# A long convolution's spectrum products shared between VectorE and GpSimd

## The chip, the cores and the metric

The kernel runs on one core of a Trainium2 chip. The metric is the device time of one execution in microseconds, the median of three runs. The kernel is one launch of three transformer-like blocks with a sequence of 512 and a model width of 1024. Below, DVE is VectorE, POOL is GpSimd, ACT is ScalarE, PE is TensorE (PEld its weight loads) and SP the queue that issues the DMAs.

## The reference

Only one step of the second block matters here, the two-sided long convolution of the Hyena mixer. It multiplies, per channel, the spectrum of `u` by the spectrum of a filter, and goes back to time:

```python
def _bidir_fftconv(u, k_fwd, k_bwd):
    L = u.shape[1]
    n = 2 * L
    D = k_fwd.shape[1]
    k_c = jnp.concatenate([k_fwd.at[0].add(k_bwd[0]), jnp.zeros((1, D), jnp.float32), k_bwd[:0:-1]], axis=0)
    kf = jnp.fft.rfft(k_c, n=n, axis=0)
    uf = jnp.fft.rfft(u, n=n, axis=1)
    return jnp.fft.irfft(uf * kf[None], n=n, axis=1)[:, :L]

# in _hyena_mixer
    u = (v * x1).astype(jnp.float32)
    y = _bidir_fftconv(u, k_fwd, k_bwd) + u * skip.astype(jnp.float32)
    y = y.astype(h.dtype) * x0
    return y @ w_out + b_out
```

## The kernel before

Everything around this step is a sequence of stages, each with a block of its own in which the five engines run their own instruction lists and meet through counting semaphores. The stage in question is `hyena_convolution` (line 2036). Its neighbours are `hyena_projection`, which makes `u` and `x0`, and the feed-forward network of the same block, which follows.

Both spectra are made by matrix products with cosine and sine tables. The filter's spectrum is already in `T.spectrum`, a tile of 128 partitions by 2 (q) by 2 (real, imaginary) by 2 (side) by 1024 channels. Even and odd samples are transformed apart, and the two sides of the spectrum are then sum and difference of the two transforms. The stage runs so:

1. PE turns `u` (line 2067), ACT copies it into `ut` (2111).
2. Four rounds n, `ROUNDS[n]` = (half, q): half picks 512 of the 1024 channels, q one of two groups of frequencies. PE makes the four parts of the unit spectrum in four banks (`parts_of_spectrum`, line 1713); rounds 0 and 2 use banks 0 to 3, rounds 1 and 3 banks 4 to 7. ACT copies the even parts out of PSUM into `even` (2118).
3. DVE does all the arithmetic of a round in `multiply(n)` (2142 to 2160). The join (2148) is two instructions that read `even` in SBUF and the odd part in PSUM and write `u`. Then, with all operands in SBUF, come four products of 128x1024 (`rr`, `ii`, `ri`, `ir`, lines 2151 to 2154), the real part `rr - ii` and the imaginary part `ri + ir` (2155, 2156), and four side sums of 128x512 (2158, 2159), which overwrite the filter's spectrum with the product's. There is one `u`, one `rr`, and so on, so the rounds follow one another.
4. PE transforms back (2083): channels 0 to 511 (tiles m of 0 to 3) when rounds 0 and 1 are finished and the join of round 2 has read its banks, channels 512 to 1023 (m of 4 to 7) when rounds 2 and 3 are finished.
5. DVE adds the skip and multiplies by `x0` (`gate`, 2166 and 2170, with `tmp` in between), ACT and DVE split the result into a high and a low part (2133, 2176), ACT and POOL split the output weights (2125, 2104), and PE makes the output product (202 to 204), whose result DVE adds to the residual (2188).

POOL does nothing in this stage but the 16 weight splits of 128x512 at line 2104. At the end of a stage, POOL clears each of its semaphores with an instruction of its own (`stage`, line 139).

Of the kernel before, what the change touches and what calls it, by code (L numbers as in the profile page):

```python
# [7 lines left out]
ALU = mybir.AluOpType  # L8
# [6 lines left out]
P = 128  # L15
SEQ = 512
D = 1024
KT = D // P
# [1680 lines left out]
HALF_D = D // 2  # L1699
# [336 lines left out]
def hyena_convolution(G, T):  # L2036
# [3 lines left out]
    with ExitStack() as ctx:  # L2040
        S = stage(G, "long", ctx, "turned", "copied", "spectra", "even_copied", "step", "joined", "product",
# [3 lines left out]
        u = G.sb("long_spectrum", [P, 2, 2, HALF_D], ctx=ctx)  # L2045
        rr, ii, ri, ir = (G.sb("long_" + n, [P, 2, HALF_D], ctx=ctx) for n in ("rr", "ii", "ri", "ir"))
        tmp = G.sb("long_tmp", [P, 4, SEQ], ctx=ctx)
        w_parts = [G.sb("long_weights_" + part, [P, 2, UNIT // 2], F32R, ctx=ctx) for part in ("high", "low")]
# [14 lines left out]
        def _(pe):  # L2063
            for t in range(KT):
                of = parity(T.uT[:, t, :])
# [11 lines left out]
            for m in range(KT):  # L2077
                if m % 4 == 0:
                    pe.wait_ge(S["joined"], 8 if m else 6)
                    pe.wait_ge(S["product"], 8 if m else 4)  # L2080
                for side in range(2):
                    for n in range(4):
                        mm = pe.matmul(G.banks[:, m, side * 256:(side + 1) * 256], T.spectrum[:, n % 2, n // 2, side, m * P:(m + 1) * P],
                                       w[:, 4 + n, side * 256:(side + 1) * 256], start=(n == 0), stop=(n == 3))
                mm.then_inc(S["back"], 1)
# [14 lines left out]
        @block.gpsimd  # L2100
        def _(pool):
            for n in range(2 * KT):
                pool.wait_ge(S["w_high"], n + 1)
                pool.tensor_tensor(w_parts[1][:, n % 2, :], landed(n), w_parts[0][:, n % 2, :].bitcast(F32), ALU.subtract)\
                    .then_inc(S["w_split"], 1)

# [32 lines left out]
        def _(dve):  # L2139
            step = Link(dve, S["step"])  # L2140

            def multiply(n):
                half, q = ROUNDS[n]
                b = 4 * (n % 2) + 2
                cols = slice(half * HALF_D, (half + 1) * HALF_D)
                dve.wait_ge(S["even_copied"], n + 1)
                for side, op in enumerate((ALU.add, ALU.subtract)):
                    dve.tensor_tensor(u[:, :, side, :], even[:, n % 2, :, :], G.banks[:, b:b + 2, :], op).then_inc(S["joined"], 1)
                dve.wait_ge(S["joined"], 2 * n + 2)
                k = T.spectrum[:, q, :, :, cols]  # L2150
                step.mark(dve.tensor_tensor(rr[:, :, :], u[:, 0, :, :], k[:, 0, :, :], ALU.mult))
                step.mark(dve.tensor_tensor(ii[:, :, :], u[:, 1, :, :], k[:, 1, :, :], ALU.mult))
                step.mark(dve.tensor_tensor(ri[:, :, :], u[:, 0, :, :], k[:, 1, :, :], ALU.mult))
                step(dve.tensor_tensor(ir[:, :, :], u[:, 1, :, :], k[:, 0, :, :], ALU.mult))
                step.mark(dve.tensor_tensor(rr[:, :, :], rr[:, :, :], ii[:, :, :], ALU.subtract))
                step(dve.tensor_tensor(ri[:, :, :], ri[:, :, :], ir[:, :, :], ALU.add))
                for side, op in enumerate((ALU.add, ALU.subtract)):
                    step.mark(dve.tensor_tensor(k[:, 0, side, :], rr[:, 0, :], rr[:, 1, :], op))
                    ins = dve.tensor_tensor(k[:, 1, side, :], ri[:, 0, :], ri[:, 1, :], op)
                    ins.then_inc(S["product"], 1)  # L2160
# [11 lines left out]
            for n in range(4):  # L2172
                multiply(n)
# [2322 lines left out]
```

## Time and profile before

| what | value |
|---|---|
| time, median of 3 runs | 4157.64 us (4155.96 to 4166.61) |
| span of the profiled execution | 4162.8 us |
| PE busy in it | 93% |
| DVE busy in it | 55% |
| POOL busy in it | 32% |
| the convolution stage, from the first turn to the last product | about 1130.7 to 1251 us |

The profiled execution is one run of its own; its span is 5.2 us above the median of the timed ones. The views used are the page (busy time per engine), the timeline (instructions of one engine in order of time; the merged ones carry a count), the view by source line (shortest, median and longest duration of a line's instructions) and the view by stretches (busy time of each engine and the granted TensorE clock in a stretch).

### The profile page before, as it was taken

How to read it: one execution, taken by the hardware profiler on the slowest of the kernel's cores; microseconds unless marked ns; L12 is line 12 of the kernel's file. 1: busy time of each engine (PE TensorE's matmuls, PEld its weight loads, DVE VectorE, ACT ScalarE, POOL GpSimd, SP SyncE). 2: the span in 40 equal slices, each digit the busy share in tenths (PEclk: the TensorE clock that was granted, in tenths of full speed). 3: DMA queues.
4: the chain of work that ended last, by engine and by line, in shares of the span. 5: the costliest groups of instructions: out<-in, count | busy, mean ns of one | idle time of the engine just before them, and what ended most of it. 6: DMA issues, size and time to landing. Idle time of an engine off the chain costs nothing. (4 is left out here: it accounts for less than half of the span.)

```text
span 4162.8 us, 63294 instructions
## 1 busy us (share of the span) xinstructions
PE 3890.4 (93%) x26374; PEld 3063.9 (74%) x26374; DVE 2293.3 (55%) x3312; ACT 1324.7 (32%) x2130; POOL 1332.2 (32%) x537
## 2 busy tenths in 40 slices
PE   8999999988989999978787999999999999999998
PEld 6855788865767887567675788877777877887886
DVE  5746477456667765558785677375550526242024
ACT  3245233233214332434444333232222111103222
POOL 1001444422314441000001344365554342663442
PEclk9999999999999999989998999999999999999998
DMA  5310222222212222341111122221212121322221
GB/s 172 122 61 22 101 81 100 105 103 81 81 41 101 101 101 102 143 169 59 44 44 65 63 101 101 101 77 72 81 61 86 56 77 53 120 96 86 83 99 61
DMA packets 43488, 361.46 MB, mean 87 GB/s; under 512 B 4355, under 2 KB 4739, under 8 KB 23916
## 3 DMA queue, kind: packets, MB, share of 16 engines
q1 hardware_dynamic: 43244, 357.95, 23.8%
q8 instruction: 184, 3.01, 0.3%
q14 instruction: 60, 0.49, 0.0%
HBM read 334.34 MB, written 23.07 MB: 86 GB/s over the span
## 5 line engine op out<-in xcount | busy, mean ns | idle before, releaser
L346 POOL TENSOR_TENSOR ffn_weights_low<-weight_ring,ffn_weights_high 128x2048 fp32r<-128x2048 f32 x128 | 591.2, 4619 | 789.9 <-ACT ffn_weights_high L443 789.2
L202 PE MATMUL banks<-ffn_in_high,ffn_weights_low 128*128 128x512 f32 x2048 | 803.8, 392 | 18.5 <-POOL ffn_weights_low L357 7.2
L203 PE MATMUL banks<-ffn_in_low,ffn_weights_high 128*128 128x512 f32 x2048 | 800.9, 391 | 0.0
L204 PE MATMUL banks<-ffn_in_high,ffn_weights_high 128*128 128x512 f32 x2048 | 800.8, 391 | 0.0
L202 PEld LDWEIGHTS banks<-ffn_in_high,ffn_weights_low 128*128 128x128 f32 x2048 | 387.2, 189 | 103.6 <-POOL ffn_weights_low L357 11.6
L204 PEld LDWEIGHTS banks<-ffn_in_high,ffn_weights_high 128*128 128x128 f32 x2048 | 386.9, 189 | 81.2
L203 PEld LDWEIGHTS banks<-ffn_in_low,ffn_weights_high 128*128 128x128 f32 x2048 | 387.3, 189 | 80.5 <-issue 0.7
L443 ACT ACTIVATE ffn_weights_high<-weight_ring 128x2048 fp32r<-128x2048 f32 x128 | 245.2, 1915 | 562.0 <-PE banks L204 562.0
L3597 POOL TENSOR_TENSOR third_weights_low<-weight_ring,third_weights_high 128x1024 fp32r<-128x1024 f32 x144 | 364.3, 2530 | 11.6
L590 DVE SCALAR_TENSOR_TENSOR ffn_gate<-ffn_up,columns_sb,ffn_gate 128x511 f32<-128x511 f32 (+1 forms) x132 | 273.5, 2072 | 160.8 <-ACT ffn_value L486 160.8
L3595 POOL CAST third_weights_high<-weight_ring 128x1024 fp32r<-128x1024 f32 x144 | 158.8, 1103 | 520.5 <-PE banks L204 484.5
L202 PE MATMUL banks<-third_x_high,third_weights_low 128*128 128x512 f32 x768 | 313.8, 409 | 7.1 <-POOLq L4013 3.9
L204 PE MATMUL banks<-third_x_high,third_weights_high 128*128 128x512 f32 x768 | 302.4, 394 | 0.0
L203 PE MATMUL banks<-third_x_low,third_weights_high 128*128 128x512 f32 x768 | 302.0, 393 | 0.0
L611 DVE TENSOR_TENSOR ffn_in_low<-ffn_hidden,ffn_in_high 128x512 fp32r<-128x512 f32 x80 | 165.9, 2121 | 138.5 <-ACT ffn_in_high L500 138.5
L3367 POOL TENSOR_TENSOR rwout_weights_low<-weight_ring,rwout_weights_high 128x1024 fp32r<-128x1024 f32 x8 | 18.6, 2354 | 655.9 <-ACT rwout_weights_high L3418 655.9
L202 PEld LDWEIGHTS banks<-third_x_high,third_weights_low 128*128 128x128 f32 x768 | 146.4, 191 | 38.1 <-issue 7.4
L204 PEld LDWEIGHTS banks<-third_x_high,third_weights_high 128*128 128x128 f32 x768 | 145.9, 190 | 31.4
L203 PEld LDWEIGHTS banks<-third_x_low,third_weights_high 128*128 128x128 f32 x768 | 146.5, 191 | 28.4 <-issue 1.0
L202 PE MATMUL banks<-first_in_high,first_weights_low 128*128 128x512 f32 x336 | 140.9, 419 | 16.1 <-DVE first_in_low L1090 12.8
L489 ACT ACTIVATE ffn_gate<-ffn_gate 128x512 f32<-128x512 f32 x66 | 41.8, 634 | 320.2 <-DVE ffn_gate L590 320.2
L3861 DVE SCALAR_TENSOR_TENSOR mlstm_conv<-mlstm_z,columns_sb,mlstm_conv 128x512 f32<-128x512 f32 x96 | 132.8, 1383 | 3.4
(609 smaller groups left out, 7386.6 us busy)
## 6 DMA issues: line engine op xcount, KB each, us to landing
weight_ring<-weights SPq DMA_DIRECT2D x144, 2048.0 KB, 7.7
scan_in<-rwkv_operands SPq DMA_DIRECT2D x7, 1280.0 KB, 6.6
rwkv_operands<-rwin_staged SPq DMA_DIRECT2D x24, 256.0 KB, 2.3
scan_in<-rwkv_operands SPq DMA_DIRECT2D x8, 512.0 KB, 4.0
bias_tiles<-bias_rows SPq DMA_DIRECT2D x8, 448.0 KB, 8.9
residual<-x SPq DMA_DIRECT2D x4, 512.0 KB, 7.0
filt_decay<-decay SPq DMA_DIRECT2D x1, 2048.0 KB, 8.2
rwkv_residual<-residual SPq DMA_DIRECT2D x1, 2048.0 KB, 7.1
```

Source lines behind the costliest of these rows:

```text
L202: pe.matmul(out, w[1], x[0], start=start, stop=False, skip_group_check=True)
L203: pe.matmul(out, w[0], x[1], start=False, stop=False, skip_group_check=True)
L204: return pe.matmul(out, w[0], x[0], start=False, stop=stop, skip_group_check=True)
L346: pool.tensor_tensor(parts[1], landed, parts[0].bitcast(F32), ALU.subtract).then_inc(S["split"], 1)
L443: act.activation(parts[0], landed, ACT.Copy).then_inc(S["rounded"], 1)
L489: act.activation(gc[:, h, :], gc[:, h, :], act_func).then_inc(S["activated"], 1)
L590: ins = dve.scalar_tensor_tensor(out=buf[:, h, to], in0=up_scaled[:, h, q, of], scalar=G.col(taps, 8 * t + 4 * q + tap), in1=buf[:, h, to] ...
L611: dve.tensor_tensor(parts[1], gT[:, t, :], parts[0].bitcast(F32), ALU.subtract).then_inc(S["tile_split"], 1)
L3367: pool.tensor_tensor(w_parts[1][:, k, :], landed(k), w_parts[0][:, k, :].bitcast(F32), ALU.subtract).then_inc(S["split"], 1)
L3595: pool.tensor_copy(parts[0], landed).then_inc(S["rounded"], 1)
L3597: pool.tensor_tensor(parts[1], landed, parts[0].bitcast(F32), ALU.subtract).then_inc(S["split"], 1)
L3861: ins = dve.scalar_tensor_tensor(out=cv[:, m, :], in0=of, scalar=G.col("m_conv", at + tap), in1=cv[:, m, :], op0=ALU.mult, op1=ALU.add)
```

## The change

It touches the convolution stage alone.

- POOL gets a part of the spectrum arithmetic ahead of its weight splits. In every round it makes `ir`, in rounds 0 to 2 `ri` too (DVE makes `ri` of round 3), and in rounds 0, 2 and 3 the two imaginary side sums (DVE makes those of round 1).
- DVE keeps the joins, `rr`, `ii`, `rr - ii`, `ri + ir` and the real side sums.
- There is a second unit spectrum, which lies in `tmp` (not in use until the gates): odd rounds write it, even rounds the old tile. So DVE joins round 2 ahead of the sums of round 1, and round 3 ahead of the sums of round 2.
- The two semaphores `step` and `product` give way to six (`real_parts`, `real_part`, `cross_parts`, `cross_part`, `real_sides`, `cross_sides`), and PE's two waits for `product` become waits for both kinds of sides.

```diff
+        u_of = lambda n: tmp.rearrange("p (r s) n -> p r s n", r=2) if n % 2 else u0
+        k_of = lambda n: T.spectrum[:, ROUNDS[n][1], :, :, ROUNDS[n][0] * HALF_D:(ROUNDS[n][0] + 1) * HALF_D]
 ...
-                    pe.wait_ge(S["product"], 8 if m else 4)
+                    pe.wait_ge(S["real_sides"], 8 if m else 4)
+                    pe.wait_ge(S["cross_sides"], 8 if m else 4)
 ...
         @block.gpsimd
         def _(pool):
-            for n in range(2 * KT):
+            def cross(n):
+                u, k = u_of(n), k_of(n)
+                pool.wait_ge(S["joined"], 2 * n + 2)
+                if n:
+                    pool.wait_ge(S["cross_part"], n)
+                pool.tensor_tensor(ir[:, :, :], u[:, 1, :, :], k[:, 0, :, :], ALU.mult).then_inc(S["cross_parts"], 1)
+                if n < 3:
+                    if n:
+                        pool.wait_ge(S["cross_sides"], 2 * n)
+                    pool.tensor_tensor(ri[:, :, :], u[:, 0, :, :], k[:, 1, :, :], ALU.mult).then_inc(S["cross_parts"], 1)
+
+            def sides(n):
+                k = k_of(n)
+                pool.wait_ge(S["cross_part"], n + 1)
+                pool.wait_ge(S["real_parts"], 2 * n + 2)
+                for side, op in enumerate((ALU.add, ALU.subtract)):
+                    pool.tensor_tensor(k[:, 1, side, :], ri[:, 0, :], ri[:, 1, :], op).then_inc(S["cross_sides"], 1)
 ...
+            cross(0)
+            sides(0)
+            cross(1)
+            cross(2)
+            sides(2)
+            cross(3)
+            sides(3)
+            for n in range(2 * KT):
+                weights(n)
 ...
         @block.vector
         def _(dve):
-            step = Link(dve, S["step"])
-
-            def multiply(n):
-                half, q = ROUNDS[n]
+            def join(n):
                 b = 4 * (n % 2) + 2
-                cols = slice(half * HALF_D, (half + 1) * HALF_D)
                 dve.wait_ge(S["even_copied"], n + 1)
+                if n >= 2:
+                    dve.wait_ge(S["cross_parts"], 2 * n - 2)
+                    dve.wait_ge(S["real_parts"], 2 * n - 2)
                 for side, op in enumerate((ALU.add, ALU.subtract)):
-                    dve.tensor_tensor(u[:, :, side, :], even[:, n % 2, :, :], G.banks[:, b:b + 2, :], op).then_inc(S["joined"], 1)
+                    dve.tensor_tensor(u_of(n)[:, :, side, :], even[:, n % 2, :, :], G.banks[:, b:b + 2, :], op).then_inc(S["joined"], 1)
+
+            def real(n):
+                u, k = u_of(n), k_of(n)
                 dve.wait_ge(S["joined"], 2 * n + 2)
-                k = T.spectrum[:, q, :, :, cols]
-                step.mark(dve.tensor_tensor(rr[:, :, :], u[:, 0, :, :], k[:, 0, :, :], ALU.mult))
-                step.mark(dve.tensor_tensor(ii[:, :, :], u[:, 1, :, :], k[:, 1, :, :], ALU.mult))
-                step.mark(dve.tensor_tensor(ri[:, :, :], u[:, 0, :, :], k[:, 1, :, :], ALU.mult))
-                step(dve.tensor_tensor(ir[:, :, :], u[:, 1, :, :], k[:, 0, :, :], ALU.mult))
-                step.mark(dve.tensor_tensor(rr[:, :, :], rr[:, :, :], ii[:, :, :], ALU.subtract))
-                step(dve.tensor_tensor(ri[:, :, :], ri[:, :, :], ir[:, :, :], ALU.add))
+                if n:
+                    dve.wait_ge(S["real_sides"], 2 * n)
+                    dve.wait_ge(S["real_part"], n)
+                dve.tensor_tensor(rr[:, :, :], u[:, 0, :, :], k[:, 0, :, :], ALU.mult).then_inc(S["real_parts"], 1)
+                dve.tensor_tensor(ii[:, :, :], u[:, 1, :, :], k[:, 1, :, :], ALU.mult).then_inc(S["real_parts"], 1)
+                dve.wait_ge(S["real_parts"], 2 * n + 2)
+                dve.tensor_tensor(rr[:, :, :], rr[:, :, :], ii[:, :, :], ALU.subtract).then_inc(S["real_part"], 1)
+
+            def cross(n):
+                if n == 3:
+                    u, k = u_of(n), k_of(n)
+                    dve.wait_ge(S["cross_sides"], 6)
+                    dve.tensor_tensor(ri[:, :, :], u[:, 0, :, :], k[:, 1, :, :], ALU.mult).then_inc(S["cross_parts"], 1)
+                dve.wait_ge(S["cross_parts"], 2 * n + 2)
+                dve.tensor_tensor(ri[:, :, :], ri[:, :, :], ir[:, :, :], ALU.add).then_inc(S["cross_part"], 1)
+
+            def sides(n, part):
+                k = k_of(n)
+                of = ri if part else rr
+                dve.wait_ge(S["cross_part"] if part else S["real_part"], n + 1)
                 for side, op in enumerate((ALU.add, ALU.subtract)):
-                    step.mark(dve.tensor_tensor(k[:, 0, side, :], rr[:, 0, :], rr[:, 1, :], op))
-                    ins = dve.tensor_tensor(k[:, 1, side, :], ri[:, 0, :], ri[:, 1, :], op)
-                    ins.then_inc(S["product"], 1)
+                    dve.tensor_tensor(k[:, part, side, :], of[:, 0, :], of[:, 1, :], op).then_inc(S["cross_sides" if part else "real_sides"], 1)
 ...
-            for n in range(4):
-                multiply(n)
+            join(0)
+            real(0)
+            cross(0)
+            sides(0, 0)
+            join(1)
+            real(1)
+            join(2)
+            cross(1)
+            sides(1, 0)
+            sides(1, 1)
+            real(2)
+            join(3)
+            cross(2)
+            sides(2, 0)
+            real(3)
+            cross(3)
+            sides(3, 0)
```

## Rows read from the trace of the kernel before

**Rows 1.** The page, first part: busy time, share of the span, instructions.

```profile
PE 3890.4 (93%) x26374; PEld 3063.9 (74%) x26374; DVE 2293.3 (55%) x3312; ACT 1324.7 (32%) x2130; POOL 1332.2 (32%) x537
```

**Rows 2.** Timeline of PE: start, length in us; in brackets idle time and its releaser.

```profile
1137.07 20.84 PE L1713 MATMUL banks<-long_u,weight_ring 128*128 128x512 f32 x48 [0.80 <-ACT long_u L2111]
1159.62 7.11 PE L1713 MATMUL banks<-long_u,weight_ring 128*128 128x512 f32 x16 [1.72 <-DVE long_spectrum L2148]
1171.39 16.61 PE L2083 MATMUL banks<-weight_ring,filter_spectrum 128*128 128x256 f32 x64 [4.66 <-DVE long_spectrum L2148]
1192.93 16.07 PE L2083 MATMUL banks<-weight_ring,filter_spectrum 128*128 128x256 f32 x64 [4.93 <-DVE filter_spectrum L2159]
```

**Rows 3.** Timeline of DVE: round 0 in part, and the end of round 3.

```profile
1145.26 2.35 DVE L2148 TENSOR_TENSOR long_spectrum<-long_even,banks 128x1024 f32<-128x1024 f32 x2 [14.87 <-ACT long_even L2118]
1147.65 1.22 DVE L2151 TENSOR_TENSOR long_rr<-long_spectrum,filter_spectrum 128x1024 f32<-128x1024 f32 x1
1148.79 1.22 DVE L2152 TENSOR_TENSOR long_ii<-long_spectrum,filter_spectrum 128x1024 f32<-128x1024 f32 x1
...
1155.32 0.69 DVE L2159 TENSOR_TENSOR filter_spectrum<-long_ri 128x512 f32<-128x512 f32 x1
1155.92 0.68 DVE L2158 TENSOR_TENSOR filter_spectrum<-long_rr 128x512 f32<-128x512 f32 x1
...
1157.13 2.35 DVE L2148 TENSOR_TENSOR long_spectrum<-long_even,banks 128x1024 f32<-128x1024 f32 x2
...
1192.10 0.69 DVE L2159 TENSOR_TENSOR filter_spectrum<-long_ri 128x512 f32<-128x512 f32 x1
```

**Rows 4.** Stretches: all engines between the first product and the last side.

```profile
1147.65:1192.79 45.14, 33.97 (x104) 21.04 (x102) 44.77 (x47) 4.10 (x5) 3.04 (x2) 0.90 0.00 0
```

**Rows 5.** By source line: POOL's subtractions, shortest, median and longest in ns.

```profile
L3367 POOL TENSOR_TENSOR rwout_weights_low<-weight_ring,rwout_weights_high x8: 2342/2354/2366, 2261.5 to 2277.7; 128x1024 fp32r<-128x1024 f32 x8
L2104 POOL TENSOR_TENSOR long_weights_low<-weight_ring,long_weights_high x16: 1259/1293/1811, 1168.4 to 1247.9; 128x512 fp32r<-128x512 f32 x16
```

**Rows 6.** Timeline: a DVE addition that starts while POOL subtracts; then its line.

```profile
1263.79 4.85 POOL L346 TENSOR_TENSOR ffn_weights_low<-weight_ring,ffn_weights_high 128x2048 fp32r<-128x2048 f32 x1 [0.18 <-POOL ffn_weights_low L357]
...
1264.09 5.11 DVE L564 TENSOR_TENSOR ffn_hidden<-ffn_hidden 128x512 f32<-128x512 f32 x1
...
L564 DVE TENSOR_TENSOR ffn_hidden<-ffn_hidden x21: 691/693/5110, 485.7 to 2358.8; 128x512 f32<-128x512 f32 x21
```

**Rows 7.** By source line: DVE and POOL instructions that run beside one another.

```profile
L557 DVE SCALAR_TENSOR_TENSOR ffn_in_low<-residual,columns_sb,ffn_in_high x24: 750/1172/1223, 476.4 to 2344.1; 128x512 fp32r<-128x512 f32 x24
L357 POOL TENSOR_TENSOR ffn_weights_low<-weight_ring,ffn_weights_high x32: 722/1078/1189, 476.0 to 3762.9; 128x256 fp32r<-128x256 f32 x32
```

**Rows 8.** Timeline: a POOL subtraction that starts within a run of DVE subtractions.

```profile
2712.56 4.90 DVE L3876 TENSOR_TENSOR third_x_low<-residual,third_x_high 128x512 fp32r<-128x512 f32 x8
...
2712.70 7.03 POOL L3597 TENSOR_TENSOR third_weights_low<-weight_ring,third_weights_high 128x1024 fp32r<-128x1024 f32 x1
```

**Rows 9.** A POOL subtraction, and the DVE line around it (2708.61 to 2712.65).

```profile
2709.27 2.37 POOL L3597 TENSOR_TENSOR third_weights_low<-weight_ring,third_weights_high 128x1024 fp32r<-128x1024 f32 x1
...
L3872 DVE SCALAR_TENSOR_TENSOR residual<-residual,columns_sb,banks x8: 743/743/748, 2707.3 to 2711.9; 128x512 f32<-128x512 f32 x8
```

**Rows 10.** Stretches: the granted clock is the third figure from the right.

```profile
1165.00:1169.70 4.70, 1.73 (x5) 0.42 (x3) 4.67 (x7) 2.06 (x3) 1.32 (x1) 1.00 0.00 0
1169.70:1176.50 6.80, 5.11 (x12) 4.13 (x13) 6.73 (x7) 0.00 (x0) 1.72 (x2) 0.50 0.01 2
1176.50:1188.00 11.50, 11.50 (x53) 9.77 (x52) 11.40 (x13) 0.00 (x0) 0.00 (x0) 1.00 0.00 0
...
1190.20:1197.00 6.80, 4.07 (x10) 3.29 (x11) 6.66 (x12) 1.26 (x2) 0.00 (x0) 0.50 0.00 0
```

**Rows 11.** By source line: POOL's clearing of the stages' semaphores.

```profile
L139 POOLq EVENT_SEMAPHORE_RANGE_CLEAR  x520: 44/44/48, 264.0 to 4162.8; - x174
```

## What the change is expected to do

> **What bounds the kernel now.** I read the page first: PE is busy for 93% of the span [rows 1], so a microsecond is won only where PE stands idle and something else decides when it goes on. Then the timeline of PE in the convolution stage. It waits three times: 1.72 us for the join of round 1 before the last forward transform, 4.66 us for the join of round 2 before the first group of back transforms, and 4.93 us for the last imaginary side of round 3 before the second group [rows 2]. The timeline of DVE shows why. After its first join it has no gap: the rounds start 11.87 us apart (1145.26, 1157.13), and the last side ends at 1192.10 + 0.69 = 1192.79, 0.14 us before PE starts its second group [rows 2, 3]. Over the 45.14 us from the first product to that side DVE is busy for 44.77, POOL for 3.04 [rows 4]. So in this stretch DVE sets the end, and what counts is the moment at which the last side of round 3 is written. PE's own work between 1145 and 1193 fits with 10 us of waits; nothing behind the second group has slack of its own (gates, weight splits and the output product start from it), so I carry a shift of that moment over to the end of the kernel one to one. In all it is a small matter: if both later waits vanished, 9.6 us or 0.23% of the time would go.
>
> **The change, part by part.** *What DVE loses.* Per round, a 128x1024 instruction comes every 1.14 us (1147.65, 1148.79) and a 128x512 one every 0.60 us [rows 3]. DVE gives away 7 of the 1024 kind and 6 of the 512 kind: 7 x 1.14 + 6 x 0.60 = 11.6 us. It keeps 17 of the 1024 kind (rr, ii, their difference and ri + ir in four rounds, and ri once), 10 of the 512 kind, and the joins, 2.35 us each [rows 3].
>
> *What POOL gains.* The trace has no POOL multiplication or addition; its subtraction of two SBUF operands takes 2.354 us at 128x1024 and 1.293 at 128x512 [rows 5]. I take these for the products and sides: 7 x 2.35 + 6 x 1.29 = 24.2 us. From below, nothing excludes a little less than that; from above see the second rival.
>
> *Whether the two run side by side.* This decides the sign. A DVE addition of two SBUF operands that takes 0.693 us takes 5.11 when it starts behind a POOL subtraction: POOL ends at 1263.79 + 4.85 = 1268.64, DVE at 1264.09 + 5.11 = 1269.20 [rows 6]. The other way round, a POOL subtraction that starts in a run of eight DVE subtractions takes 7.03 us, and ends 2.27 after the run ends (2719.73 against 2712.56 + 4.90 = 2717.46) [rows 8]. Where both engines have a string of such work, each is slowed: 0.75 to 1.17 us at the median on DVE, 0.72 to 1.08 on POOL [rows 7]. So a DVE instruction with both inputs in SBUF and a POOL one exclude one another. A DVE instruction with an input from PSUM is free of it: line 3872 never takes over 0.748 us though a POOL subtraction runs beside several of its eight [rows 9]. All that is left to DVE here but the joins has both inputs in SBUF; the joins read a bank.
>
> The Trainium skill (SBUF — State Buffer, Who interferes with whom) speaks against this change in the same sense: a two-input DVE instruction and a GpSimd instruction that reads SBUF contend for one shared read interface, and the later one blocks until the other is finished. The rows agree, but for one point: in rows 8 POOL waited for eight instructions, not for one. With a strict turn after every instruction none of joins 2 and 3 would be hidden, and the sum below would come out near +8 us.
>
> *The sum.* Exclusive time of one instruction is its length less what runs ahead of its turn. For DVE, 0.56 us at 512 (1269.20 - 1268.64), so 0.13 less than alone, and 1.22 - 0.13 = 1.09 at 1024 [rows 3, 6]. For POOL, 2.27 at 1024, 0.08 less than alone, and 1.29 - 0.08 = 1.21 at 512 [rows 5, 8]. From the first product to the last side:
> DVE 17 x 1.09 + 10 x 0.56 = 24.1; POOL 7 x 2.27 + 6 x 1.21 = 23.2; together 47.3 us of which no two can overlap. Before, the same stretch took 45.1, with 7.05 us of three joins in it [rows 3, 4]. So even if all three joins vanish beside POOL's work, the last side comes 47.3 - 45.1 = 2.2 us later; if none does, 9.2 us later. The work taken from DVE costs twice as much on POOL, and the exclusion leaves no parallel time to pay for it but the joins.
> Join 1 lies beside POOL's sides of round 0 in any order: hidden. Join 2 comes behind the difference of round 1, and is hidden if POOL then still has ri of round 1 to make, which depends on whether DVE keeps its turn through rr and ii (as in rows 8) or POOL comes in between (as in rows 7). Join 3 stands to round 2 as join 2 to round 1. I take one of the two as hidden: 47.3 + 2.35 = 49.7. To it come the changes of engine where neither works, about 0.15 us from a POOL product to DVE's addition and back, some six or seven times: about 1 us. 50.7 - 45.1 = +5.6 us.
>
> *New waits and what is queued behind them.* DVE's addition ri + ir waits for POOL's two products; behind it stand the real sides, and in round 0 join 1, for which PE's last forward transform waits. That transform moves by about 1 us (its start was 1159.62), and its result is next needed for join 3, past 1175: covered. Join 2 waits for the products of round 0, done long before. On POOL the first two weight splits, at 1168.38 before, now stand behind all cross work and are done some 3 us after the last side, 13 us before the output product wants them: nothing. SP's first load waits for the last back transform and moves with it; its later ones wait for the ninth split onwards: nothing. PE's first group needs the sides of round 1; it may start as late as 1198.4 - 16.6 = 1181.8 without holding up the second, and I expect 1172 to 1178: covered [rows 2]. The second unit spectrum costs no instruction.
>
> *The clock.* Behind the pause at 1166.7 the granted clock fell from 1.00 to 0.50, that is from 2.4 to 1.2 GHz, for 6.8 us, and behind the pause at 1188 again [rows 10]. The second group ran its first 4.1 us at the lower level, worth half, 2.0 us. The pause ahead of it will be longer or its start fall elsewhere; no half-speed stretch in these rows is longer than 6.8 us, so the loss lies between 0 and 3.4 us: a difference of -2.0 to +1.4. I take 0. In the first group the loss is hidden by DVE.
>
> *The end of the stage.* Six semaphores for two make four more clears on POOL, 44 ns each [rows 11]. POOL's first work of the next stage follows them directly, and PE waits for it there: 4 x 0.044 = +0.2.
>
> Sum: 5.6 + 0 + 0.2 = +5.8 us. On the profiled span of 4162.8 this would be 4168.6; on the median of the timed runs, 5.2 lower, 4157.6 + 5.8 = 4163.4. A measurement of this kernel can tell a difference of about 0.3%, 12.5 us, from none.
>
> **The rivals.** *(a) The two engines do run side by side.* For it: DVE alone would need 4 x (2.35 + 3 x 1.14 + 1.14 + 1.2) + 1.14 + 1.2 = 34.8 us instead of 47.5, and POOL's 24.2 fit under that; DVE waiting for POOL's products would take back some 3. The last side would come 9 to 10 us earlier, with a second group at full clock up to 13: 4145 to 4149. Against it: rows 6 to 8. They are subtractions and additions with fp32r outputs in part, but line 564 is plain fp32. It needs the exclusion to be absent here: 0.07.
> *(b) POOL's products are dearer than its subtractions.* Each microsecond that a 128x1024 product takes over 2.35 is paid seven times in exclusive time, for DVE cannot work beside it. From 3.35 us a product (+7 us) the sum passes 12.5 us and the kernel is measurably slower: 4170 to 4180. Nothing in the trace shows a POOL product; line 2104 with a longest of 1.811 [rows 5] shows only what a turn lost costs. 0.06.
> *(c) DVE keeps its turn more often, and all joins are hidden.* Only 2 to 3 us later: 4160. It is inside my forecast's range.
> *(d) The work is moved but the order doesn't matter*, because PE's first group becomes the bound: it would have to start past 1181.8. With strict turns and 20% dearer POOL work it comes near 1180, not past it. It adds nothing by itself.
>
> **How the numbers follow.** Forecast (exclusive turns, +0 to +12 us with the bounds of joins, clock and clears): 0.87, of which 0.03 lies above 12.5 us. Rival (a): 0.07, about 0.03 of it under -12.5 us, when clock and overlap both come out well. Rival (b): 0.06, four fifths of it above 12.5. Faster by over 0.3%: 0.03. Slower: 0.03 + 0.05 = 0.08. Within 0.3%: 0.89. The range: the sum without hidden losses is +2.2 - 2.0 = 0.2, with everything against it 9.2 + 1 + 0.3 + 1.4 = 11.9, which gives 4158 to 4170; three runs before spread over 10 us (4155.96 to 4166.61), so their median can be off by some 3, and I take 4154 to 4173. This leaves out (a) and the upper part of (b), 0.13.
>
> **What the profile after would show.** DVE instructions of rr, ii, sides that take 1.22 and 0.69 us now would show lengths of 2.2 to 3.5 us beside POOL's, while the joins keep 1.22. POOL's products would show 2.35 when alone and more when DVE has the turn. The last side would be written at about 1198, and PE's wait before its second group would be 7 to 10 us instead of 4.93, with the first group starting at 1172 to 1178. DVE's busy time in the stretch would go up, not down, though it does 11.6 us less work. I am wrong if products stand beside one another at 1.22 and 2.35; if join 1 does not lie beside POOL's sides; or if a POOL product alone takes more than 3 us.

## The result and the profile after

| | before | after |
|---|---|---|
| time, median of 20 runs | 4157.57 us | 4165.79 us |
| ratio of after to before | | 1.0017, 95% interval 1.0009 to 1.0025 |
| span of the profiled execution | 4162.8 us | 4167.1 us |
| first product to last side | 45.1 us | 53.2 us |
| PE's pause ahead of the second group | 4.93 us | 8.42 us |
| first turn of the stage to first product of the next | 125.4 us | 132.8 us |

The changed kernel is 0.17% slower, which is 4 to 10 us; the stage alone, read from the two traces, is 7.4 us longer (from 1130.71 to 1256.11 before, from 1131.45 to 1264.28 after). The two spans differ by 4.3 us only: the stages that the change doesn't touch were together 3.1 us shorter in the profiled execution of the changed kernel.

The timeline of DVE in the changed kernel, rounds 0 and 1 (start, length, both in us; compare with [rows 3]):

```profile
1148.39 1.23 DVE L2186 TENSOR_TENSOR long_rr<-long_spectrum,filter_spectrum 128x1024 f32<-128x1024 f32 x1
1149.54 3.37 DVE L2187 TENSOR_TENSOR long_ii<-long_spectrum,filter_spectrum 128x1024 f32<-128x1024 f32 x1
1152.94 3.25 DVE L2189 TENSOR_TENSOR long_rr<-long_rr,long_ii 128x1024 f32<-128x1024 f32 x1
1156.11 1.21 DVE L2197 TENSOR_TENSOR long_ri<-long_ri,long_ir 128x1024 f32<-128x1024 f32 x1
1157.25 2.35 DVE L2204 TENSOR_TENSOR filter_spectrum<-long_rr 128x512 f32<-128x512 f32 x2
1159.52 2.34 DVE L2178 TENSOR_TENSOR long_tmp<-long_even,banks 128x1024 f32<-128x1024 f32 x2
...
1166.43 3.25 DVE L2189 TENSOR_TENSOR long_rr<-long_rr,long_ii 128x1024 f32<-128x1024 f32 x1
1169.61 2.34 DVE L2178 TENSOR_TENSOR long_spectrum<-long_even,banks 128x1024 f32<-128x1024 f32 x2
...
1183.23 2.34 DVE L2178 TENSOR_TENSOR long_tmp<-long_even,banks 128x1024 f32<-128x1024 f32 x2
```

The same for POOL, all its spectrum work; the brackets give its idle time and what ended it:

```profile
1148.44 3.38 POOL L2110 TENSOR_TENSOR long_ir<-long_spectrum,filter_spectrum 128x1024 f32<-128x1024 f32 x1 [35.95 <-DVE long_spectrum L2178]
1151.79 3.32 POOL L2114 TENSOR_TENSOR long_ri<-long_spectrum,filter_spectrum 128x1024 f32<-128x1024 f32 x1
1157.40 3.32 POOL L2121 TENSOR_TENSOR filter_spectrum<-long_ri 128x512 f32<-128x512 f32 x2 [2.29 <-DVE long_ri L2197]
1161.94 3.38 POOL L2110 TENSOR_TENSOR long_ir<-long_tmp,filter_spectrum 128x1024 f32<-128x1024 f32 x1 [1.21 <-DVE long_tmp L2178]
1165.28 3.32 POOL L2114 TENSOR_TENSOR long_ri<-long_tmp,filter_spectrum 128x1024 f32<-128x1024 f32 x1
1173.23 2.65 POOL L2110 TENSOR_TENSOR long_ir<-long_spectrum,filter_spectrum 128x1024 f32<-128x1024 f32 x1 [4.62 <-DVE long_ri L2197]
1177.71 3.26 POOL L2114 TENSOR_TENSOR long_ri<-long_spectrum,filter_spectrum 128x1024 f32<-128x1024 f32 x1 [1.83 <-DVE filter_spectrum L2204]
...
1186.79 3.32 POOL L2121 TENSOR_TENSOR filter_spectrum<-long_ri 128x512 f32<-128x512 f32 x2 [5.82 <-DVE long_ri L2197]
1190.08 3.33 POOL L2110 TENSOR_TENSOR long_ir<-long_tmp,filter_spectrum 128x1024 f32<-128x1024 f32 x1
1198.23 3.32 POOL L2121 TENSOR_TENSOR filter_spectrum<-long_ri 128x512 f32<-128x512 f32 x2 [4.82 <-DVE long_ri L2197]
```

Read the two side by side. `rr` runs from 1148.39 to 1149.62 and is not disturbed. POOL's `ir` was issued at 1148.44 and ends at 1151.82, 2.20 us after `rr`. `ii` was issued at 1149.54 and ends at 1152.91, 1.09 us after `ir`. `ri` ends 2.20 us after `ii`, and the difference ends 1.08 us after `ri`. So, but for some 0.1 us at the start of each, no two of them overlap. Nothing else is slow: the joins keep 2.34 us for two, also the first, half of which runs beside POOL's sides.

PE in the two stretches (the rows that answer to the last two of [rows 2]), and the stretch from first product to last side (as [rows 4]: length, busy time of PE, PEld, DVE, ACT, POOL, granted clock):

```profile
1177.78 15.49 PE L2086 MATMUL banks<-weight_ring,filter_spectrum 128*128 128x256 f32 x64 [8.67 <-DVE filter_spectrum L2204]
1201.70 15.48 PE L2086 MATMUL banks<-weight_ring,filter_spectrum 128*128 128x256 f32 x64 [8.42 <-POOL filter_spectrum L2121]
...
1148.39:1201.55 53.16, 32.85 (x104) 20.28 (x102) 52.82 (x35) 4.11 (x5) 32.52 (x14) 0.90 0.00 0
```

DVE is busy for 52.8 us with 35 instructions where it was busy for 44.8 with 47. Both of PE's later pauses have become longer, and the second is now ended by POOL.

### The profile page after: what moved, and what is told of

It is laid out like the page before. It is cut to its first block and busy times, and to the rows that moved or that the text cites. A ratio compares the mean times of both kernels' runs of the same rounds, so it can differ in the third digit from the quotient of the medians.

```text
span 4167.1 us, 63309 instructions
## 1 busy us (share of the span) xinstructions
PE 3888.9 (93%) x26374; PEld 3062.8 (73%) x26374; DVE 2299.4 (55%) x3299; ACT 1324.7 (32%) x2130; POOL 1365.3 (33%) x550
## 5 line engine op out<-in xcount | busy, mean ns | idle before, releaser
L3921 DVE SCALAR_TENSOR_TENSOR mlstm_conv<-mlstm_z,columns_sb,mlstm_conv 128x512 f32<-128x512 f32 x96 | 132.8, 1383 | 3.4
```

What stands on the lines that cost most here:

```text
L3921: ins = dve.scalar_tensor_tensor(out=cv[:, m, :], in0=of, scalar=G.col("m_conv", at + tap), in1=cv[:, m, :], op0=ALU.mult, op1=ALU.add)
```

## The experiments

The theory: a POOL instruction that reads SBUF and a DVE instruction with both inputs in SBUF exclude one another, so work moved from DVE to POOL is added up, not overlapped, and costs about twice as much there. The main rival: what costs is the chain of hand-overs (DVE, POOL, DVE, POOL in each round), whatever the engines read. Smaller questions: the price of a product on POOL, and what the new order is worth. The measure of a single effect is the stretch from the start of the first product to the end of the last side, since single executions differ by some microseconds in stages that have nothing to do with it. Each stretch is read from one profiled execution. e2_joins_in_place, e3_pool_writes_only and e4_bystander were run once only, so they have no ratio.

| kernel | stretch, us | ratio to before (95%) |
|---|---|---|
| before | 45.1 | |
| after | 53.2 | 1.0017 (1.0009 to 1.0025) |
| e1_order_only | 46.0 | 1.0001 (0.9989 to 1.0013) |
| e2_joins_in_place | 52.2 | |
| e3_pool_writes_only | 33.1 | |
| e4_bystander | 64.2 | |
| e5_beside_joins | 44.1 | 0.9994 (0.9982 to 1.0006) |
| e6_unit_in_psum | 39.5 | 0.9976 (0.9966 to 0.9986) |
| e7_join_beside_product | 49.7 | 1.0011 (0.9999 to 1.0023) |
| e8_psum_rebalanced | 36.3 | 0.9971 (0.9956 to 0.9986) |

**GpSimd writes, but reads nothing.** Against the changed kernel:

```diff
-                pool.tensor_tensor(ir[:, :, :], u[:, 1, :, :], k[:, 0, :, :], ALU.mult).then_inc(S["cross_parts"], 1)
+                pool.memset(ir[:, :, :], 0.0).then_inc(S["cross_parts"], 1)
-                    pool.tensor_tensor(ri[:, :, :], u[:, 0, :, :], k[:, 1, :, :], ALU.mult).then_inc(S["cross_parts"], 1)
+                    pool.memset(ri[:, :, :], 0.0).then_inc(S["cross_parts"], 1)
-                    pool.tensor_tensor(k[:, 1, side, :], ri[:, 0, :], ri[:, 1, :], op).then_inc(S["cross_sides"], 1)
+                    pool.memset(k[:, 1, side, :], 0.0).then_inc(S["cross_sides"], 1)
```

> The changed kernel, with GpSimd's products and side sums replaced by fills of the same tiles, which read nothing; order, waits and VectorE's work are as in the changed kernel, and the spectrum's imaginary part is not computed. Theory (two-input VectorE work and GpSimd work that reads exclude one another on a read path): rr, ii and rr - ii of 128x1024 all last 1.22 us and the sides 0.69, none stretched, even where a fill runs beside them, and the last side comes 9 to 12 us earlier than before (45.1 us from first product to last side becomes 33 to 36). Rival (any GpSimd instruction stretches VectorE's, or only the hand-overs between the engines cost): ii stays at 2 to 3.4 us, or the lengths are normal but the stretch stays at 45 us or more.

Timelines of POOL and DVE of this kernel, round 1:

```profile
1148.13 0.95 POOL L2110 MEMSET long_ir<- 128x1024 f32 x1 [2.47 <-DVE long_tmp L2178]
1149.02 0.95 POOL L2114 MEMSET long_ri<- 128x1024 f32 x1
...
1148.11 1.23 DVE L2186 TENSOR_TENSOR long_rr<-long_tmp,filter_spectrum 128x1024 f32<-128x1024 f32 x1
1149.25 1.22 DVE L2187 TENSOR_TENSOR long_ii<-long_tmp,filter_spectrum 128x1024 f32<-128x1024 f32 x1
1150.50 1.23 DVE L2189 TENSOR_TENSOR long_rr<-long_rr,long_ii 128x1024 f32<-128x1024 f32 x1
```

The same order and the same waits, and no DVE instruction is stretched, though the fills lie right beside `rr` and `ii`. The stretch is 33.1 us. A fill lasts 0.95 us and not 2.35, so this kernel doesn't tell what a hand-over costs with slower work. But it is 20.0 us shorter than the changed kernel, and the whole of this is in the lengths of DVE's instructions: DVE is busy for 32.8 us of the stretch instead of 52.8, and idle for 0.3 us in either.

**A bystander.** The kernel before, with POOL's share of the arithmetic added on tiles that nobody needs; nothing is taken from DVE:

```diff
+            for n in range(7):
+                pool.wait_ge(S["idle_work"] if n else S["joined"], n or 2)
+                pool.tensor_tensor(tmp[:, 0:2, :], ut[:, 0:2, 0:512], ut[:, 2:4, 0:512], ALU.mult).then_inc(S["idle_work"], 1)
+            for n in range(6):
+                pool.wait_ge(S["idle_work"], 7 + n)
+                pool.tensor_tensor(tmp[:, 0, :], ut[:, 0, 0:512], ut[:, 2, 0:512], ALU.mult).then_inc(S["idle_work"], 1)
```

> The kernel before, with 7 GpSimd multiplications of 128x1024 and 6 of 128x512 added from the first join on, on tiles that nobody waits for before the gates: the GpSimd work of the change without its hand-overs and without relief for VectorE. Theory (exclusion): from first product to last side the 45.1 us grow by the GpSimd work that falls in it and does not lie beside a join, 23 us less up to 7, so 61 to 68 us, and single VectorE instructions last 1.09 us beyond the end of a GpSimd one. Rival (hand-overs cost the time, not the sharing): 45 to 46 us, VectorE's lengths unchanged. Second question, the price of a GpSimd product: where one waits for nobody it should last 2.35 us at 128x1024; if products were dearer than subtractions it would be over 2.6.

Timeline of POOL, and of DVE, three of the products and two of the sides of round 0:

```profile
1140.87 22.55 POOL L2104 TENSOR_TENSOR long_tmp<-long_u 128x1024 f32<-128x1024 f32 x7 [34.52 <-DVE long_spectrum L2154]
...
1141.96 3.37 DVE L2158 TENSOR_TENSOR long_ii<-long_spectrum,filter_spectrum 128x1024 f32<-128x1024 f32 x1
1145.26 3.37 DVE L2159 TENSOR_TENSOR long_ri<-long_spectrum,filter_spectrum 128x1024 f32<-128x1024 f32 x1
1148.55 3.36 DVE L2160 TENSOR_TENSOR long_ir<-long_spectrum,filter_spectrum 128x1024 f32<-128x1024 f32 x1
...
1163.88 1.75 DVE L2164 TENSOR_TENSOR filter_spectrum<-long_rr 128x512 f32<-128x512 f32 x1
1165.55 1.75 DVE L2165 TENSOR_TENSOR filter_spectrum<-long_ri 128x512 f32<-128x512 f32 x1
```

The stretch grows by 19.1 us to 64.2, though in it neither engine's arithmetic waits for the other's once POOL has started behind the first join. That is the exclusion alone. A DVE product comes every 3.29 us, one of its own turns (1.09) and one of POOL's (2.20), so a product costs POOL 2.20 us of exclusive time. This is no more than the 2.27 worked out for a subtraction from [rows 8]; rival (b) of the prediction has no ground. Two sides that met POOL's 128x512 work come 1.67 us apart, 0.56 for DVE and 1.11 for POOL, where the prediction had put 1.21. Every product at 128x1024 met DVE's work, so its undisturbed length, which the expectation asked for, is not shown; it follows only as 2.20 us and what runs ahead of the turn.

**The order alone.** Second unit tile and early joins, all arithmetic on DVE:

```diff
+                if n:
+                    dve.wait_ge(S["cross_part"], n)
+                    dve.wait_ge(S["cross_sides"], 2 * n)
+                dve.tensor_tensor(ir[:, :, :], u[:, 1, :, :], k[:, 0, :, :], ALU.mult).then_inc(S["cross_parts"], 1)
+                dve.tensor_tensor(ri[:, :, :], u[:, 0, :, :], k[:, 1, :, :], ALU.mult).then_inc(S["cross_parts"], 1)
...
             cross(0)
             sides(0, 0)
+            sides(0, 1)
```

> The second unit spectrum and the joins of rounds 2 and 3 ahead of the sums of rounds 1 and 2, as in the changed kernel, but all arithmetic on VectorE. Theory: VectorE is busy without a gap either way, so the last side comes within 1 us of where it came before (45.1 us from first product to last side, 0 to 1 more for the added waits); time within 0.05% of before. Rival (the order is what brings or costs the time): more than 3 us of change in the stretch.

Timelines of DVE and POOL, the real sides of round 1 and the first two weight splits:

```profile
1168.07 3.42 DVE L2180 TENSOR_TENSOR filter_spectrum<-long_rr 128x512 f32<-128x512 f32 x2
...
1167.86 3.08 POOL L2107 TENSOR_TENSOR long_weights_low<-weight_ring,long_weights_high 128x512 fp32r<-128x512 f32 x2 [56.40 <-ACT long_weights_high L2131]
```

46.0 us, 0.9 more than before, and no difference in time. The exclusion costs more than these 0.9 us: POOL's first two weight splits met two real sides, which took 3.42 us instead of 1.29, where before they had lain mostly beside a join. Without these 2.1 us the stretch would be about 43.9. So the new order saves some 1.2 us, because an instruction no longer stands directly behind the one whose result it needs (before, the difference starts 1.26 us after `ir`, at 1151.06 and 1152.32; here it starts 1.13 us after `ri`, at 1150.79 and 1151.92), and the splits take more than that back. As built, the order brings nothing.

**The joins back in place, POOL's share kept.** Against the changed kernel:

```diff
-        u_of = lambda n: tmp.rearrange("p (r s) n -> p r s n", r=2) if n % 2 else u0
+        u_of = lambda n: u0
...
-                    dve.wait_ge(S["cross_parts"], 2 * n - 2)
-                    dve.wait_ge(S["real_parts"], 2 * n - 2)
+                    dve.wait_ge(S["cross_parts"], 2 * n)
+                    dve.wait_ge(S["real_parts"], 2 * n)
...
             real(1)
-            join(2)
             cross(1)
             sides(1, 0)
             sides(1, 1)
+            join(2)
             real(2)
-            join(3)
             cross(2)
             sides(2, 0)
+            join(3)
             real(3)
```

> The changed kernel with GpSimd's share as it is, but one unit spectrum tile and every join where it was, behind the sums of the round before. Theory: the early joins of rounds 2 and 3 hid nothing in the changed kernel, since GpSimd had no product left beside them, so first product to last side stays at 52.5 to 54.5 us. Rival (the early join brings something): over 55 us.

52.2 us, one less than the changed kernel and just under what was expected. The early join didn't fail to help, it did harm: in its old place the join of round 3 runs beside POOL's sides of round 2, in the new one beside nothing.

**The joins ahead of the difference.** One step earlier still:

```diff
                 dve.tensor_tensor(ii[:, :, :], u[:, 1, :, :], k[:, 1, :, :], ALU.mult).then_inc(S["real_parts"], 1)
+                if n < 3:
+                    join(n + 1)
                 dve.wait_ge(S["real_parts"], 2 * n + 2)
```

> The changed kernel with one thing moved: VectorE joins round n + 1 after rr and ii of round n and ahead of their difference, so that the join, which reads PSUM, falls where GpSimd still has its second product to make. Theory (exclusive turns; in the changed kernel only 1.2 of 7.05 us of joins lay beside GpSimd's reading work): the joins now lie beside GpSimd's products, first product to last side falls from 53.2 us to 47.3 to 49, and the time from about 7 us over the kernel before to 2 to 4 us over it. Rival (the loss is the length of the chain of hand-overs, which this leaves as it is): 52 to 54 us.

Timeline of DVE around the join of round 2, and POOL's product beside it:

```profile
1156.00 3.36 DVE L2187 TENSOR_TENSOR long_ii<-long_tmp,filter_spectrum 128x1024 f32<-128x1024 f32 x1
1159.29 2.34 DVE L2178 TENSOR_TENSOR long_spectrum<-long_even,banks 128x1024 f32<-128x1024 f32 x2
1161.55 1.21 DVE L2191 TENSOR_TENSOR long_rr<-long_rr,long_ii 128x1024 f32<-128x1024 f32 x1
...
1158.25 3.34 POOL L2114 TENSOR_TENSOR long_ri<-long_tmp,filter_spectrum 128x1024 f32<-128x1024 f32 x1
```

The join now lies wholly beside `ri`, and the difference behind it is back at 1.21 us from 3.25. The stretch falls to 49.7 us, against 47.3 to 49 expected: joins 1 and 2 are hidden, join 3 (1172.79 to 1175.13) is not, since POOL's second product of round 2 had to wait for the sides of round 1 and was over at 1171.79. This speaks against the chain of hand-overs as the cause, for the chain is the same. The time, 0.11% over before with an interval that just reaches no difference, lies a little above the expected 2 to 4 us.

**POOL only beside the joins.** Against the kernel before:

```diff
+            for n in range(3):
+                half, q = ROUNDS[n]
+                k = T.spectrum[:, q, :, :, half * HALF_D:(half + 1) * HALF_D]
+                pool.wait_ge(S["sums"], 2 * n + 2)
+                for side, op in enumerate((ALU.add, ALU.subtract)):
+                    pool.tensor_tensor(k[:, 1, side, :], ri[:, 0, :], ri[:, 1, :], op).then_inc(S["product"], 1)
```

> The kernel before, with one thing given to GpSimd: the two imaginary side sums of rounds 0 to 2, released after VectorE's real sides so that they run beside the next round's join. Theory (a two-input GpSimd instruction is free only beside VectorE work that reads PSUM): three times 1.2 us leave VectorE, GpSimd's 2.4 us lie beside the join's 2.35 and cost rr some 0.3 us of waiting; first product to last side 42 to 43.5 us instead of 45.1, time 1.5 to 3 us under before, at the limit of what 5 rounds tell. Rival (hand-overs eat it): 45 us or more.

Timelines of DVE and POOL at the end of round 1, and then in round 3:

```profile
1165.72 2.35 DVE L2155 TENSOR_TENSOR long_spectrum<-long_even,banks 128x1024 f32<-128x1024 f32 x2
1168.10 1.36 DVE L2158 TENSOR_TENSOR long_rr<-long_spectrum,filter_spectrum 128x1024 f32<-128x1024 f32 x1
...
1165.88 2.50 POOL L2108 TENSOR_TENSOR filter_spectrum<-long_ri 128x512 f32<-128x512 f32 x2 [8.29 <-DVE filter_spectrum L2167]
...
1180.18 2.29 DVE L2159 TENSOR_TENSOR long_ii<-long_spectrum,filter_spectrum 128x1024 f32<-128x1024 f32 x1
1182.39 2.28 DVE L2162 TENSOR_TENSOR long_ri<-long_spectrum,filter_spectrum 128x1024 f32<-128x1024 f32 x1
...
1179.14 4.45 POOL L2111 TENSOR_TENSOR long_weights_low<-weight_ring,long_weights_high 128x512 fp32r<-128x512 f32 x2
```

Each round does get shorter: the joins of rounds 1 and 2 start 10.79 us apart (1154.93, 1165.72) instead of 11.87. But the stretch falls by 1.1 us only, to 44.1, missing the 42 to 43.5. The cause stands in the last three lines: POOL's first two weight splits, now later, met `ii` and `ri` of round 3, which follow one another at 2.21 us instead of 1.14. That is 2.1 us; without it the stretch would be 41.9, at the low end of what was expected. The time can't be told from that of the kernel before.

**The unit spectrum in PSUM.** If the exclusion is one of reading two tiles of SBUF, it is to be avoided by giving DVE's products an input in PSUM. The joins write the unit spectrum back into the four banks of its round, and POOL makes the sums of one round beside the products of the next:

```diff
+        second = [tmp[:, 0:2, :], tmp[:, 2:4, :], u0[:, 0, :, :], u0[:, 1, :, :]]
+        sets = [[t[:, :, :] for t in (rr, ii, ri, ir)], second]
+        u_of = lambda n: G.banks[:, 4 * (n % 2):4 * (n % 2) + 4, :].rearrange("p (s r) n -> p r s n", r=2)
...
+                    dve.tensor_tensor(G.banks[:, b + 2 * side:b + 2 * side + 2, :], even[:, n % 2, :, :], G.banks[:, b + 2:b + 4, :], op)\
...
+                for out, a, b in ((rr, 0, 0), (ii, 1, 1), (ri, 0, 1), (ir, 1, 0)):
+                    dve.tensor_tensor(out, u[:, a, :, :], k[:, b, :, :], ALU.mult).then_inc(S["parts"], 1)
...
+            for n in range(3):
+                real(n)
+                cross(n)
+                sides(n)
+            real(3)
```

Here `real`, `cross` and `sides` are POOL's `rr - ii`, `ri + ir` and real sides; PE's transforms of rounds 2 and 3 wait for the products of rounds 0 and 1.

> The same arithmetic shared so that the engines do not meet on the read path: the joins write the unit spectrum back into its own four banks of PSUM, so that VectorE's four products of a round have one input in PSUM; GpSimd makes rr - ii, ri + ir and the real sides of rounds 0 to 2 and rr - ii of round 3 beside them; products have two sets of tiles. Theory (exclusion holds only for VectorE instructions with both inputs in SBUF): all 16 products last 1.22 us, GpSimd's sums beside them 2.35, the last side comes 10 to 14 us earlier than in the kernel before, and with PE's pauses shorter the time is 10 to 15 us (0.25 to 0.35%) under it. Rival (GpSimd work stretches VectorE's whatever it reads): products of 2 to 3.4 us, last side as in the changed kernel or later, no gain.

The lines of DVE's products and of POOL's difference (shortest, median and longest in ns), one of each from the timelines, and the stretch:

```profile
L2184 DVE TENSOR_TENSOR long_tmp<-banks,filter_spectrum x4: 1214/1220/1225, 1147.9 to 1170.0; 128x1024 f32<-128x1024 f32 x4
L2110 POOL TENSOR_TENSOR long_rr<-long_rr,long_ii x2: 2358/2358/2359, 1143.4 to 1160.9; 128x1024 f32<-128x1024 f32 x2
...
1143.21 1.22 DVE L2184 TENSOR_TENSOR long_ri<-banks,filter_spectrum 128x1024 f32<-128x1024 f32 x1
1143.37 2.36 POOL L2110 TENSOR_TENSOR long_rr<-long_rr,long_ii 128x1024 f32<-128x1024 f32 x1 [38.35 <-DVE long_ii L2184]
...
1140.94:1180.45 39.51, 31.19 (x97) 18.98 (x96) 39.41 (x34) 4.11 (x5) 28.82 (x15) 0.91 0.00 0
```

Both engines run at their undisturbed lengths, 1.22 and 2.36 us, side by side. The stretch is 39.5 us, 5.6 less than before and 13.7 less than in the changed kernel, and the whole kernel is 0.24% faster than before. That is just under the expected gain in time (its interval, 0.14 to 0.34%, is 6 to 14 us; in the trace the stage, from the first turn to the next stage's first product, is 6.2 us shorter), and the stretch missed its 10 to 14 us by half. What is missing are the sums left to DVE, which still meet POOL: the imaginary sides of rounds 0, 1 and 2 took 3.74, 3.55 and 2.49 us a pair instead of 1.29, and the sum `ri + ir` of round 3 took 2.28 instead of 1.22. That is 7.0 us in all, and 5.6 + 7.0 = 12.6.

**The same, with more given to POOL.**

```diff
+                if n:
+                    ri = sets[n % 2][2]
+                    pool.wait_ge(S["cross_part"], n + 1)
+                    for side, op in enumerate((ALU.add, ALU.subtract)):
+                        pool.tensor_tensor(k[:, 1, side, :], ri[:, 0, :], ri[:, 1, :], op).then_inc(S["cross_sides"], 1)
...
             products(2)
-            sides(1, 1)
             join(3)
             products(3)
```

> The version with the unit spectrum in PSUM, with more given to GpSimd: all of round 1 and 2 behind the products (difference, sum and four sides), of round 0 all but the imaginary sides; VectorE makes the sums of round 3 alone. Theory (exclusive turns only for two-SBUF-input work): VectorE runs the joins and products of rounds 2 and 3 without sums between them; last side some 3 to 4 us earlier than the 39.5 us of the first such version (35.5 to 37), the first group of back transforms starts about 5 us earlier, PE goes through both groups with a pause under 2 us, and the time is 13 to 17 us under the kernel before. Rival (GpSimd becomes the bound, its chain of 9.7 us a round ends later than VectorE's): stretch 39 us or more, time as the first version, about 10 us under before.

Timeline of POOL, its last sides, and of PE in both groups:

```profile
1173.46 2.49 POOL L2129 TENSOR_TENSOR filter_spectrum<-long_ri 128x512 f32<-128x512 f32 x2
...
1168.58 29.52 PE L2091 MATMUL banks<-weight_ring,filter_spectrum 128*128 128x256 f32 x128 [3.37 <-DVE long_ir L2191]
```

36.3 us, in the middle of what was expected. POOL is not the bound: its last side of round 2 is written at 1175.95, DVE's last side at 1182.73. PE goes through both groups in one piece, as it did in e6_unit_in_psum too, with one pause of 3.37 us before them where I had written under 2 (6.93 there). Counted from the first turn, its first group starts 3.6 us earlier than in e6_unit_in_psum, not the expected 5. From the first turn to the next stage's first product the stage takes 115.7 us, 9.7 less than before. The time, 0.29% or 12 us under before (0.14 to 0.44%), falls just short of the 13 to 17 us that I had written and can't be told from that of e6_unit_in_psum. Both versions beat both kernels.

## Why the prediction was right

The forecast was 4163.4 us, +5.8; measured were 4165.8, and by the ratio +7 us (4 to 10). The sign and the mechanism hold: the work that POOL took over is added to DVE's. The size is less good than the time makes it look. The stretch was to grow by 5.6 us and grew by 8.0. The joins cost 3.5 us more than forecast, POOL's work 1.1 less; that these two partly cancelled, and that the clock gave 0.6 back, was luck.

- **The exclusive sum** of 47.3 us comes out of the trace to a tenth, but not from the terms that I gave. In the changed kernel the joins lay beside POOL's reading work for 1.20 of 7.0 us (join 1, from 1159.52 until POOL's sides ended at 1160.72), so 5.8 us stood alone, and 53.16 - 5.8 = 47.3. In these 47.3 POOL's share is not 23.2 us: its products end 2.20 us after the DVE instruction before them and not 2.27, its sides 1.11 and not 1.21 (e4_bystander), so 7 x 2.20 + 6 x 1.11 = 22.1. With DVE's 24.1 that makes 46.2, and 1.1 to 1.2 us are left for the next term. Carried over as a whole, the 47.3 also gives e7_join_beside_product (two joins hidden, 47.3 + 2.35 = 49.7, measured 49.7) and e2_joins_in_place (joins 1 and 3 half hidden, 52.0, measured 52.2).
- **The hidden joins** were the term that was mis-sized. I had counted join 1 and one of joins 2 and 3 as hidden, 2.35 us left alone; it was 5.8. Join 1 is hidden only in half, because DVE's real sides and POOL's imaginary ones take turns first (2.35 and 3.32 us for two each). Join 2 (1169.61) starts when POOL has been idle since 1168.60, and join 3 (1183.23) since 1180.97. After every DVE instruction POOL had its turn, so both products were over by the time DVE reached the join. The Trainium skill (SBUF — State Buffer, Who interferes with whom) calls what the two engines share an exclusive lock. The trace agrees: each of these instructions ends its own exclusive time (1.09 or 2.20 us) after the one of the other engine. The strict turn, which the prediction had put at near +8, gave +8.0; to the tenth this is luck as well, since join 1, which that sum took as hidden, cost 1.1 us, and POOL's price was 1.1 us too high. I had leaned on [rows 8], where POOL waited for a whole run, and those rows didn't carry over.
- **The hand-overs** were put at 1 us. They are what the 47.3 us hold beyond 46.2, 1.1 to 1.2 us: the term was right. They lie where the engine changes or an instruction waits for the one just before it, as in the 1.23 us of `rr` after a join, where 1.09 is its exclusive time.
- **The clock.** The difference was taken as 0. From the last side to the first output product were 15.9 us before (1192.79 to 1208.65) and 15.3 after (1201.55 to 1216.83), so 0.6 us in favour of the change, within the bounds given (from -2.0 to +1.4). The clock was granted at 0.50 (1.2 GHz) for the group's first 4.1 us before [rows 10]; after, it was at 1.00 (2.4 GHz) again at the latest 4.3 us into the group, and in part from 2.3 us on. If the 0.85 of the middle row is a mean of 0.50 and 1.00, the lower level lasted about 2.9 us instead of 4.1, and half of that difference is the 0.6 us (an estimate from these rows):

```profile
1201.70:1204.00 2.30, 2.30 (x6) 1.85 (x7) 2.27 (x4) 0.82 (x2) 2.30 (x2) 0.50 0.00 0
1204.00:1206.00 2.00, 2.00 (x9) 1.74 (x8) 1.97 (x3) 0.44 (x1) 0.92 (x1) 0.85 0.00 0
1206.00:1217.00 11.00, 11.00 (x53) 9.69 (x51) 5.65 (x9) 0.00 (x0) 0.00 (x0) 1.00 0.01 2
```

- **The semaphore clears** were to cost 0.2 us. From first output product to the next stage's first product are 47.46 us before and 47.45 after: nothing.
- **Covered items.** PE's first group started at 1177.78 (I wrote 1172 to 1178) and was over at 1193.3, before the last side at 1201.55: covered. The forward transform of round 3 waited 3.36 us instead of 1.72 and delayed nobody. The weight splits came in time for the output product.
- **The rivals.** (a), no exclusion, fell in the trace and in e4_bystander. (b), dearer products, fell in e4_bystander. (c), more joins hidden, is the opposite of what happened. Of the signs that I had named for the profile after, most appeared: `ii` at 3.37 us, joins at 1.21 each, PE's pause of 8.42 us, and DVE busier with fewer instructions. Join 1, however, lay beside POOL's sides for half its length only, and the last side was written at 1201.55 and not at about 1198; 0.74 us of that are a later start of the whole stage.

What stays open is why POOL got its turn between `rr` and `ii`, when neither had been held up before, while in [rows 8] it waited for eight DVE instructions in a row. No run was made for it. Nor does any of these stretches hold a POOL instruction with a single input in SBUF, so it stays open whether such a one excludes DVE too.

## What to carry to other kernels

Before elementwise work goes from VectorE to GpSimd, look at where the inputs lie: if both of VectorE's inputs are in SBUF and GpSimd reads two from SBUF too, the two add up, and since GpSimd takes twice as long (2.20 us against 1.09 here, for a product of 128x1024 in fp32) the kernel loses. An engine that shows 7% busy in a stretch is no spare capacity by that alone; one instruction of the one kind that starts within one of the other, somewhere in the same trace, tells it. Split the work so that VectorE's share has an input in PSUM (a result may be written back into the banks that it came from, as in e6_unit_in_psum), and lay the rest of GpSimd's work beside that.

## What the runs showed of the hardware that I had not expected

- Turns were strict in this stage: after each DVE instruction of 1.09 us of exclusive time came a POOL one of 2.20, also where DVE's next instruction had been issued back to back (`ii` at 1149.54, `rr` ending at 1149.62).
- POOL fills of 128x1024 (0.95 us) run beside two-input DVE instructions without lengthening them; it is not POOL's writing that excludes.
- POOL's own weight splits, two instructions of 1.3 us that were harmless before because they lay mostly beside a join, cost DVE up to 2.1 us as soon as another order put them beside its sums.
